# Mamba-2 block with a grouped top-2 mixture of experts: experts and last stage in the same block as the projection, norm rows and eight residual tiles loaded beside the last expert tiles

## Chip, cores, metric

One core of a Trainium2 chip. The metric is the device time of one launch in microseconds; the kernel before was run three times. A profiled execution goes with it.

## What is computed

One decoder layer over 2048 tokens of 1024 features, float32. The part that the change touches is the end of it:

```python
x = layer_norm(ALPHA * x + (1 + g1) * y, ln_g[0], ln_b[0])     # y: the mixer's result times w_out
hm = x * (1 + sc2) + sh2
probs = softmax(hm @ w_router + b_router)                      # 32 experts in 4 groups
# the best group by the sum of its two best; in it the two best experts, gates scaled to sum 1
ye = (silu(hm @ w_gate[e]) * (hm @ w_up[e])) @ w_down[e]       # for both experts of each token
y = gate_a * ye_a + gate_b * ye_b
out = layer_norm(ALPHA * x + (1 + g2) * y, ln_g[1], ln_b[1])
```

Every float32 product is made of three products of rounded parts: a matrix is split into a high part (cast by ScalarE) and a low part (what is left, subtracted by VectorE or GpSimd).

## The kernel before

The program is a row of blocks. In a block each engine (TensorE pe, VectorE dve, ScalarE act, GpSimd pool, and the DMA queue of SyncE, sp) has a list of instructions of its own, with semaphore waits between them written out by hand; at a block's end all engines meet. `stage` (L101) builds a stage and then has GpSimd clear, one by one, every semaphore that the stage took, in a block of its own (`clear_semaphores`, L90). There are three stages.

*Stage 1, `mixer_steps`:* 32 steps of the mixer, then in the same block `out_projection` (L1470). It goes over 16 token tiles of 128. On TensorE a step i does the first half of tile i's product (24 matmuls), the turn of tile i-1 (8 transposes, L1579), the second half, and the router product of tile i-1 (L1591). In the last step the turn comes behind the second half. VectorE's `tile` (L1720 to L1747) scales the product (L1727), adds x (L1731), takes the statistics, and makes the router's input h2 from the normed row (L1745, L1747); GpSimd takes the power for the deviation and makes ALPHA times the normed row (L1554, L1556), which ScalarE stores as the residual tile (L1678, `k.xad`), after which SyncE loads the next tile of x into the same buffer. `choose` is the routing: a chain of some 40 small VectorE instructions with one exponential on ScalarE (`power`), called for tiles 0 to 12 (`choose(0, ...)`) and for 13 to 15. TensorE's `rank` then counts, by products with a triangle and with ones, the place of each token in its expert. The router products of tiles 13 and later write the bank that choose(0) reads, so they wait for it:

```python
if isinstance(j, int) and j >= EARLY:
    pe.wait_ge(p_ready, 1)
```

`p_ready` is counted up by choose's third instruction (L1807).

*Stage 2, `experts`:* VectorE works out the plan from the ranks (L2152, nt_i, and on): which token goes to which place of which tile of 128. TensorE turns it into lists of tokens (L2023). GpSimd gathers the tokens of a tile by indirect DMA (L1945), and for each of 46 tiles TensorE makes gate and up products (L1983), turns the result (L2014) and makes the down product. The weights of an expert come in six pieces of 1 MB (gate 0, 1; up 2, 3; down 4, 5), each with a raw buffer, a high part (L2040, ScalarE) and a low part (L1933; pieces 3 and 5 by GpSimd, the others by VectorE). A piece is loaded again once its low part is made. The results are stored by ScalarE (L2052).

*Stage 3, `output`:* for each of 16 token tiles GpSimd gathers both experts' rows (L2257, two indirect DMAs), SyncE loads the residual tile (L2234), in rings of 8; ScalarE scales and squares, VectorE adds, norms and scales (L2299 to L2332), GpSimd takes the power (rstd, L2267), SyncE stores (L2243). GpSimd issues the 16 gathers of the first 8 tiles ahead of the first power.

Of the kernel before, what the change touches and what calls it, by code (L numbers as in the profile page):

```python
# [47 lines left out]
BY_POOL = (0, 2)  # L48

# [146 lines left out]
def mixer_steps(nc, k, first):  # L196

    with ExitStack() as ctx:
        own = ExitStack()
# [61 lines left out]
        o = projection_buffers(k, ctx, first)  # L261
# [31 lines left out]
        def heads_of(row):  # L293
# [15 lines left out]
                 "t1_done y_done yn_done sq_done xdt_done xend_done xd_done y3 gt ms_done rs_done").split())  # L309
        block = ctx.enter_context(nc.Block())  # L310
# [774 lines left out]
        def _(dve):  # L1085
# [378 lines left out]
        out_projection(nc, k, o, block, first, Tail(  # L1464
            ymm=(ymm, SUBS * STEPS), yn_tr=(yn_tr, 2 * STEPS), y_done=(y_done, 2 * STEPS), gt=(gt, 2 * STEPS),
            yt_out=(yt_out, 2 * STEPS), gm_done=(gm_done, STEPS),
            y_stored=[(y, 32 * STEPS) for y in y_stored]))


def out_projection(nc, k, o, block, first, tail):  # L1470


    sem = k.semaphore
    HALF = YTILES // 2
    w_hi, w_lo, yraw, yhi, ylo, wraw = o.w_hi, o.w_lo, o.yraw, o.yhi, o.ylo, o.wraw
# [8 lines left out]
    row_in, mix = sem("row_in"), sem("mix")  # L1484
    eq = flat[:, 0:NE]
    gs, gh, i1 = (flat[:, (2 * E + n * EGROUPS) * EARLY:(2 * E + (n + 1) * EGROUPS) * EARLY] for n in range(3))
    rb_in, p_ready, exp_done, eq_ready, pos_mm, chain = (sem(n) for n in (
        "rb_in p_ready exp_q eq_ready pos_mm chain_q").split())
    (wr_in, t_done, r_done, bn_done, mv_done, ve_done, rstd_done, nmr_done,
     xn_done, xa_out, ha_done, h2_done, h2_out, tr_done, ht_done, lg_mm, xm_done, xa_done) = (sem(n) for n in (  # L1490
         "wr_in t_done r_done bn_done mv_done ve_done rstd_done nmr_done "
         "xn_done xa_out ha_done h2_done h2_out trh_done ht_done lg_mm xm_done xa_done").split())
    x_in = sem("xo_in")
# [19 lines left out]
    def _(sp):  # L1513
# [30 lines left out]
        loop(sp, step)  # L1544

    @block.gpsimd
    def _(pool):
        def step(i, b):
# [7 lines left out]
            nc.gpsimd.tensor_tensor(r[:], r[:], k.b1[:], ALU.add).then_inc(xa_done, 1)  # L1556

        loop(pool, step)

    @block.tensor  # L1560
    def _(pe):
# [33 lines left out]
        def step(i, b):  # L1595
# [49 lines left out]
    def _(act):  # L1645
# [11 lines left out]
        def step(i, b):  # L1657

            j = i - 1
            if in_loop(j, 0, TT):  # L1660
# [20 lines left out]
            if isinstance(i, int) and i == TT - 2:  # L1681
                power(0, EARLY)
# [7 lines left out]
        act.wait_ge(xa_out, 16 * TT)  # L1690
        act.wait_ge(h2_out, 16 * TT)

    @block.vector
    def _(dve):
# [135 lines left out]

        loop(dve, step, 1)
        choose(1, EARLY, TT - EARLY)
        dve.wait_ge(pos_mm, 2)


def experts(nc, k, first):

    with ExitStack() as ctx:
        sb, ps, sem = k.makers(ctx)
        FQ = FE // P
        GU = 4
        PIECES = GU + 2
        raw = [sb(f"piece_raw{q}", [P, 4, 512]) for q in range(PIECES)]
        hi = [sb(f"piece_hi{q}", [P, 4, 512], F32R) for q in range(PIECES)]
        lo = [sb(f"piece_lo{q}", [P, 4, 512], F32R) for q in range(PIECES)]
        ix = [sb(f"ix{b}", [P, 1], I32) for b in range(2)]
# [118 lines left out]
        def _(pe):  # L1968
# [30 lines left out]
            def step(t, b):  # L1999
# [8 lines left out]
                if in_loop(t, 1):  # L2008
                    down(t - 1)
# [452 lines left out]
```

## Time and profile before

| | us |
|---|---|
| median of 3 runs (lowest, highest) | 2989.3 (2984.44, 2990.38) |
| profiled execution, its own time | 2990.43 |
| its span, first to last instruction | 2988.6 |
| TensorE busy | 2718.9 (91%) |
| VectorE, ScalarE, GpSimd busy | 2218.1, 1315.9, 1489.7 |
| projection, tile 1's products to the last rank | 1542 to 1965 |
| experts, plan to last product | 1975 to 2865 |
| last stage, first gather to last instruction | 2873 to 2983 |

Times in rows are microseconds from the span's start; the duration of a row with a count is that of the group. An "idle before" with a releaser is what the engine waited for. A block's end, a branch and a semaphore clear have no row; they show as a gap on all engines. The semaphores' hardware numbers are given out again in a later stage.

### The profile page before, as it was taken

The page shows a single profiled execution, that of the slowest core. Times are in us where ns is not written, and L with a number is a line of the kernel's source. Part 1 is how long each engine was busy: PE and PEld are TensorE (multiplying, and loading weights), DVE is VectorE, ACT ScalarE, POOL GpSimd, SP SyncE. Part 2 cuts the span into 40 slices and gives each one's busy share as a digit, 9 for nine tenths or more (in the row PEclk, how much of TensorE's full clock was granted, in tenths as well). Part 3 has the DMA queues.
Part 4 walks back from the last instruction along what each step waited for, and adds up shares of the span by engine and source line. Part 5 has one row for each costly group of instructions (what it writes and reads, how often), then busy time and mean ns, then how long its engine had stood idle before and what let it go on. Part 6 is the DMA issues. An engine that isn't in the chain of part 4 may idle for free. (4 is left out here: it accounts for less than half of the span.)

```text
span 2988.6 us, 41030 instructions
## 1 busy us (share of the span) xinstructions
PE 2718.9 (91%) x14603; PEld 2316.1 (77%) x14603; DVE 2218.1 (74%) x2647; ACT 1315.9 (44%) x1655; POOL 1489.7 (50%) x755
## 2 busy tenths in 40 slices
PE   3899999999999999999979999949999999999920
PEld 2688888888889888888868888747888888888820
DVE  7678777777878777887863333458888888888857
ACT  4443333343433333343431111126777777777733
POOL 0133433343343334334432222126899999999963
PEclk9899999999999999999989999959999999999965
DMA  8844544444553544455252322249878869678676
GB/s 271 310 183 145 211 155 171 174 171 161 184 211 137 190 175 165 166 184 197 95 169 106 105 105 105 78 152 373 319 269 293 307 242 341 233 259 288 245 273 247
DMA packets 253185, 610.13 MB, mean 204 GB/s; under 512 B 15968, under 2 KB 98560, under 8 KB 244864
## 3 DMA queue, kind: packets, MB, share of 16 engines
q1 hardware_dynamic: 228208, 525.26, 49.2%
q0 software_dynamic: 11520, 41.95, 3.7%
q10 hardware_dynamic: 13328, 41.21, 3.4%
q8 instruction: 79, 1.29, 0.2%
q14 instruction: 50, 0.41, 0.0%
HBM read 600.75 MB, written 99.89 MB: 234 GB/s over the span
## 5 line engine op out<-in xcount | busy, mean ns | idle before, releaser
L1933 DVE TENSOR_TENSOR piece_lo<-piece_raw,piece_hi 128x2048 fp32r<-128x2048 f32 x187 | 563.3, 3031 | 102.5 <-ACT piece_hi L2040 101.3
L2040 ACT CAST piece_hi<-piece_raw 128x2048 fp32r<-128x2048 f32 x280 | 526.7, 1910 | 217.8 <-issue 77.8
L1933 POOL TENSOR_TENSOR piece_lo<-piece_raw,piece_hi 128x2048 fp32r<-128x2048 f32 x93 | 558.9, 6010 | 34.5 <-ACT piece_hi L2040 32.3
L574 PE MATMUL op<-hm,w_hi 128*128 128x512 f32 x2048 | 533.4, 406 | 45.2 <-DVE hm L1236 45.2
L1110 DVE SCALAR_TENSOR_TENSOR cv<-ub,par,cv 128x512 f32<-128x512 f32 x384 | 381.0, 992 | 157.1 <-ACT cv L833 147.9
L574 PEld LDWEIGHTS op<-hm,w_hi 128*128 128x128 f32 x2048 | 379.8, 190 | 119.5 <-DVE hm L1236 45.2
L524 POOL TENSOR_TENSOR xw<-xw,t 128x512 f32<-128x512 f32 x64 | 98.7, 1543 | 488.6 <-DVE t L1178 488.5
L589 PE MATMUL pz<-wz_hi,hm 128*128 128x256 f32 x2048 | 296.9, 290 | 1.1 <-DVE wz_lo L1088 0.5
L589 PEld LDWEIGHTS pz<-wz_hi,hm 128*128 128x128 f32 x2048 | 266.8, 192 | 7.4 <-DVE wz_lo L1088 3.9
L574 PE MATMUL op<-hm,w_lo 128*128 128x512 f32 x1024 | 254.9, 391 | 0.0
L505 POOL TENSOR_TENSOR xdt<-xw,tab 128x512 f32<-128x512 f32 x64 | 70.4, 1100 | 369.3 <-ACT xw L852 345.1
L574 PEld LDWEIGHTS op<-hm,w_lo 128*128 128x128 f32 x1024 | 192.4, 188 | 42.9
L1983 PE MATMUL gp_e<-piece_lo,xt_hi 128*128 128x512 f32 x368 | 151.7, 412 | 4.1 <-DVE xt_lo L2093 4.1
L1983 PE MATMUL yp<-piece_lo,ht_hi 128*128 128x512 f32 x368 | 150.0, 407 | 6.0 <-DVE ht_lo L2128 6.0
L1945 POOL DMA_INDIRECT xg<-hm,ix x48 | 127.7, 2660 | 39.0 <-POOL ix L1942 39.0
L1983 PE MATMUL gp_e<-piece_hi,xt_hi 128*128 128x512 f32 x368 | 146.8, 399 | 0.0
L1983 PE MATMUL gp_e<-piece_hi,xt_lo 128*128 128x512 f32 x368 | 146.5, 398 | 0.0
L1983 PE MATMUL yp<-piece_hi,ht_lo 128*128 128x512 f32 x368 | 146.1, 397 | 0.0
L1983 PE MATMUL yp<-piece_hi,ht_hi 128*128 128x512 f32 x368 | 145.9, 397 | 0.0
L1983 PE MATMUL up_e<-piece_lo,xt_hi 128*128 128x512 f32 x368 | 145.5, 395 | 0.0
L1983 PE MATMUL up_e<-piece_hi,xt_hi 128*128 128x512 f32 x368 | 145.5, 395 | 0.0
L1550 POOL TENSOR_TENSOR rstd<-ve,negh 128x1 f32<-128x1 f32 x16 | 8.8, 550 | 274.2 <-DVE ve L1740 274.2
(338 smaller groups left out, 5698.2 us busy)
## 6 DMA issues: line engine op xcount, KB each, us to landing
hm<-hm_parts SPq DMA_DIRECT2D x30, 4096.0 KB, 13.9
piece_raw<-in_w_gate SPq DMA_DIRECT2D x94, 1024.0 KB
piece_raw<-in_w_up SPq DMA_DIRECT2D x94, 1024.0 KB
piece_raw<-in_w_down SPq DMA_DIRECT2D x92, 1024.0 KB
decay<-acum_rows SPq DMA_DIRECT2D x32, 1024.0 KB
w_raw<-in_w_in SPq DMA_DIRECT2D x48, 512.0 KB, 7.5
expert_out<-ye ACTq DMA_DIRECT2D x46, 512.0 KB
w_ada_part<-in_w_ada_t SPq DMA_DIRECT2D x32, 512.0 KB, 3.9
```

Of the source, the lines that this page charges most:

```text
L505: nc.gpsimd.tensor_tensor(heads(xdt, h), heads(xw, h), k.tab[:, 0, part].unsqueeze(2).to_broadcast([P, 2 * RH, HD]), ALU.mult).then_inc(xd ...
L524: nc.gpsimd.tensor_tensor(x, x, t1[h][:], ALU.add).then_inc(y3, 1)
L574: mm = nc.tensor.matmul(pj[m % 2][:], wp[m][:, kk, :], hm[b][:, hp, kk, :], start=q == 0, stop=q == 3 * KK - 1)
L589: mm = nc.tensor.matmul(pz[:, (a % 2) * GW:(a % 2 + 1) * GW], hm[b][:, hp, kk, a * P:(a + 1) * P], wp[:, kk, :], start=q == 0, stop=q == 3 ...
L1110: nc.vector.scalar_tensor_tensor(out=cv[m % 2][:], in0=ub[:, m, t:t + SPAN], scalar=par[:, t:t + 1], in1=cv[m % 2][:], op0=ALU.mult, op1=A ...
L1550: nc.gpsimd.tensor_tensor(rstd[:], ve[:], k.negh[:, 0:1], ALU.pow).then_inc(rstd_done, 1)
L1933: v.tensor_tensor(lo[q][:], raw[q][:], hi[q][:].bitcast(F32), ALU.subtract).then_inc(lo_done[q], 1)
L1945: nc.gpsimd.indirect_dma_start(out=xg[b][:], out_offset=None, in_=k.h2d[:], in_offset=bass.IndirectOffsetOnAxis(ap=ix[b][:], axis=0)).then ...
L1983: mm = nc.tensor.matmul(acc[:], l[:, first + kk, :], r[:, kk, :], start=start and kk == 0 and n == 0, stop=stop and kk == 3 and n == 2)
L2040: nc.scalar.copy(hi[q][:], raw[q][:]).then_inc(hi_done[q], 1)
```

## The change

One block holds projection, experts and last stage. Their buffers are placed by hand so that each lies where what was there before is done with, and their semaphores live side by side. The mixer's 93 own semaphores are cleared by GpSimd in tile 1 of the projection, to be given out again to the experts and the last stage; everything is cleared once more at the end of the stage.

- SyncE loads the first tile's six weight pieces once the last product of the projection is done, then the row g2. ScalarE makes their high parts around tile 15 and the routing, VectorE the low parts 0 and 1 ahead of choose(1) and 2 behind it, GpSimd 3 and 5.
- choose(0) moves behind tile 14 on VectorE (from step 14 to step 15), its exponential behind a wait for tile 13's router product on ScalarE.
- The turn of tile 0 on TensorE moves behind the second half of tile 1.
- SyncE loads the last stage's two norm rows and residual tile 0 ahead of the expert loop, tiles 1 to 7 as the last expert tile's low parts free their places. The gathers go once all expert results are stored.

The diff, cut:

```diff
+def output_buffers(k, ctx):
...
+    xa = [sb(f"xa{n}", [P, D]) for n in range(1, OUT_RING)]
...
@@ mixer_steps
+        k.semaphores, kept = own_sems, len(k.used)
...
+        of_mixer = k.used[kept:]
+        k.semaphores = stay
+        out_sems = projection_semaphores(k)
+        own_sems.close()
+        of_experts = ExitStack()
+        x = experts_buffers(k, of_experts)
+        of_experts.close()
+        w = output_buffers(k, ctx)
...
+        experts(nc, k, x, o, w, block, first, out_sems, out)
@@ out_projection, sync
         loop(sp, step)
+        sp.wait_ge(o_mm, 2 * TT)
+        for q in range(x.PIECES):
+            sp.dma_start(x.raw[q][:], first_weights(k, q)).then_inc(x.loaded[q], 16)
+        sp.wait_ge(xm_done, TT)
+        sp.dma_start(x.g2[:], k.adad[3].partition_broadcast(P)).then_inc(x.g2_in, 16)
@@ gpsimd
+            if not in_loop(i, 2) and in_loop(i, 1):
+                for s in of_mixer:
+                    pool.sem_clear(s)
         loop(pool, step)
+        for q in (3, 5):
+            pool.wait_ge(x.hi_done[q], 1)
+            nc.gpsimd.tensor_tensor(x.lo[q][:], x.raw[q][:], x.hi[q][:].bitcast(F32), ALU.subtract
+                                    ).then_inc(x.lo_done[q], 1)
@@ tensor
-            final = isinstance(i, int) and i == TT - 1
-            if before and not final:
+            behind = isinstance(i, int) and i in (1, TT - 1)
+            if before and not behind:
                 turn(i - 1)
             if here:
                 products(b, 1)
-            if final:
+            if behind:
                 turn(i - 1)
@@ scalar
                 act.dma_start(k.h2d[bass.ds(j * P, P), :], h2[:]).then_inc(h2_out, 16)
+                if isinstance(j, int) and j == TT - 1:
+                    first_high(0)
+                    first_high(1)
                 if in_loop(j, 1, TT):
                     act.wait_ge(lg_mm, j)
+                if isinstance(j, int) and j == TT - 2:
+                    power(0, EARLY)
...
                 if isinstance(j, int) and j == TT - 1:
                     power(1, TT - EARLY)
+                    first_high(3)
+                    first_high(2)
...
-            if isinstance(i, int) and i == TT - 2:
-                power(0, EARLY)
+        def first_high(q):
+            act.wait_ge(x.loaded[q], 16)
+            nc.scalar.copy(x.hi[q][:], x.raw[q][:]).then_inc(x.hi_done[q], 1)
...
         loop(act, step, 1)
-        act.wait_ge(xa_out, 16 * TT)
-        act.wait_ge(h2_out, 16 * TT)
+        first_high(5)
+        first_high(4)
@@ vector
             if in_loop(i, 1):
                 tile(i - 1, 1 - b)
+            if isinstance(i, int) and i == TT - 1:
+                choose(0, 0, EARLY)
             if in_loop(i, 1, TT - 1):
                 low(i + 1, 1 - b)
             if not in_loop(i, 1):
                 mix_rows()
-            if isinstance(i, int) and i == TT - 2:
-                choose(0, 0, EARLY)
...
         loop(dve, step, 1)
+        first_low(0)
+        first_low(1)
         choose(1, EARLY, TT - EARLY)
+        first_low(2)
         dve.wait_ge(pos_mm, 2)
@@ experts, sync
+        sp.wait_ge(x_in[0], 16)
+        sp.wait_ge(ids_mm, 1)
+        for row, source in ((w.lng, k.d["ln_g"][1]), (w.lnb, k.d["ln_b"][1])):
+            sp.dma_start(row[:], source.partition_broadcast(P)).then_inc(w.row_in, 16)
+        sp.wait_ge(arrived.xa_out, 16 * TT)
+        sp.dma_start(w.xa[0][:], k.xad[0]).then_inc(w.xa_in[0], 16)
+        last = loop(sp, step)
+        for n in range(1, OUT_RING):
+
+            if n % 2:
+                sp.wait_ge(lo_done[(n - 1) // 2], 2 * last + 3)
+                sp.sem_inc(k.passed, 1)
+            sp.dma_start(w.xa[n][:], k.xad[n]).then_inc(w.xa_in[n], 16)
@@ gpsimd
+        for b in range(2):
+            pool.wait_ge(ye_out[b], 16 * (last + 1))
+            pool.sem_inc(k.passed, 1)
@@ program
-            stage(nc, k, mixer_steps, first)
-            if stop > 2:
-                stage(nc, k, experts, first)
-        if stop > 4:
-            stage(nc, k, output, out)
+            stage(nc, k, mixer_steps, first, out)
```

Where it moves instructions. VectorE behind the low parts of tile 15, before (h and r are the projection's rows, yraw here holds the routing's scores, lgP the router's sums):

```order
L1697 TENSOR_TENSOR ylo1a<-yraw,yhi1a 128x1024 [waits yhi_done]
L1697 TENSOR_TENSOR ylo1b<-yraw,yhi1b 128x1024 [waits yhi_done]
L1805 TENSOR_TENSOR yraw<-lgP,rb 128x416 [waits ylo_done,rb_in,lg_mm]
L1806 TENSOR_REDUCE mx<-yraw 128x13 [waits chain_q]
L1807 TENSOR_TENSOR yraw<-yraw,mx 128x416 [waits chain_q]
L1809 TENSOR_REDUCE sm<-yraw 128x13 [waits exp_q]
```

and in the changed kernel:

```order
L1851 TENSOR_TENSOR h<-op,g 128x512 [waits o_mm]
L1855 SCALAR_TENSOR_TENSOR r<-r,h 128x1024 [waits t_done,xo_in]
L1859 BN_STATS bst<-r 128x6 [waits r_done]
L1859 BN_STATS bst<-r 128x6
L1862 BN_AGGR mv<-bst 128x2 [waits bn_done]
L1864 TENSOR_SCALAR ve<-mv 128x1 [waits mv_done]
L1866 SCALAR_TENSOR_TENSOR nmr<-mv,rstd 128x1 [waits rstd_done]
L1869 TENSOR_TENSOR h<-r,wo_raw 128x1024 [waits xn_done]
L1871 TENSOR_TENSOR h<-h,wo_raw 128x1024 [waits ha_done]
L1929 TENSOR_TENSOR yraw<-lgP,rb 128x416 [waits ylo_done,rb_in,lg_mm]
L1930 TENSOR_REDUCE mx<-yraw 128x13 [waits chain_q]
L1931 TENSOR_TENSOR yraw<-yraw,mx 128x416 [waits chain_q]
```

All ten instructions of tile 14 now stand ahead of the routing, and with them ahead of the third row of it, which counts p_ready.

ScalarE from tile 15's normed row on, before:

```order
L1662 ACTIVATE r<-r,nmr,rstd 128x1024 [waits nmr_done]
L1666 DMA hm<-h 128x1024 [waits h2_out,h2_done]
L1673 COPY h2t<-tp 128x512 [waits trh_done,lg_mm]
L1673 COPY h2t<-tp 128x512 [waits trh_done]
L1687 ACTIVATE yraw<-yraw 128x96 [waits p_ready]
L1678 DMA alpha_x<-r 128x1024 [waits xa_done]
L198 UNCONDITIONAL_BRANCH [waits h2_out,xa_out]
L2034 UNCONDITIONAL_BRANCH [waits barrier_Pool_Activation_PE_DVE_SP_release]
```

and in the changed kernel:

```order
L1777 ACTIVATE r<-r,nmr,rstd 128x1024 [waits nmr_done]
L1781 DMA hm<-h 128x1024 [waits h2_out,h2_done]
L1806 CAST piece_hi<-piece_raw 128x2048 [waits w_loaded0]
L1806 CAST piece_hi<-piece_raw 128x2048 [waits w_loaded1]
L1793 COPY h2t<-tp 128x512 [waits trh_done,lg_mm]
L1793 COPY h2t<-tp 128x512 [waits trh_done]
L1811 ACTIVATE yraw<-yraw 128x96 [waits p_ready]
L1806 CAST piece_hi<-piece_raw 128x2048 [waits w_loaded3]
L1806 CAST piece_hi<-piece_raw 128x2048 [waits w_loaded2]
L1800 DMA alpha_x<-r 128x1024 [waits xa_done]
L1806 CAST piece_hi<-piece_raw 128x2048 [waits w_loaded5]
L1806 CAST piece_hi<-piece_raw 128x2048 [waits w_loaded4]
```

Two casts of weight pieces stand ahead of the copies of the turned tile 15, two between the exponential and the residual store, two behind it.

GpSimd at the end of the program, before (ISA is here a semaphore clear; a name behind "waits" is that of the first semaphore with that number):

```order
L2267 TENSOR_TENSOR rstd<-ve,negh 128x1 [waits stm_done,y_done] x8
L2212 UNCONDITIONAL_BRANCH
L94 UNCONDITIONAL_BRANCH [waits barrier_Pool_Activation_PE_DVE_SP_gather]
L97 ISA x36
L92 UNCONDITIONAL_BRANCH
```

and in the changed kernel:

```order
L2375 TENSOR_TENSOR rstd<-ve,negh 128x1 [waits y_stored0,c_th] x8
L279 UNCONDITIONAL_BRANCH
L95 UNCONDITIONAL_BRANCH [waits barrier_Pool_Activation_PE_DVE_SP_gather]
L98 ISA x221
L93 UNCONDITIONAL_BRANCH
```

The rows of 137 and of 48 clears that stood at the two boundaries are gone; the last one has 221.

## Rows read from the trace of the kernel before

**Rows 1.** Page of the profile, part 1: busy us and share of the span by engine.
```profile
PE 2718.9 (91%) x14603; PEld 2316.1 (77%) x14603; DVE 2218.1 (74%) x2647; ACT 1315.9 (44%) x1655; POOL 1489.7 (50%) x755
```

**Rows 2.** Timeline from 1902 us: start, us, engine, line, operation, count, idle time before.
```profile
1902.72 2.01 PE L1566 MATMUL op<-wo_hi,ylo0b 128*128 128x512 f32 x8
1903.57 0.59 DVE L1805 TENSOR_TENSOR yraw<-lgP,rb 128x416 f32<-128x416 f32 x1
...
1905.56 1.94 PE L1591 MATMUL lgP<-w_router,h2t 128*128 128x32 f32 x16 [0.83 <-DVE yraw L1807]
...
1920.45 1.29 DVE L1727 TENSOR_TENSOR h<-op,g 128x512 f32<-128x512 f32 x2
...
1929.77 1.03 PE L1579 MATMUL tp<-ident,h 128*128 128x128 f32 x8
```

**Rows 3.** Timeline, VectorE in a token tile of the steady state.
```profile
1879.90 0.69 DVE L1727 TENSOR_TENSOR h<-op,g 128x512 f32<-128x512 f32 x1 [0.67 <-PE op L1566]
...
1887.20 1.22 DVE L1747 TENSOR_TENSOR h<-h,wo_raw 128x1024 f32<-128x1024 f32 x1
```

**Rows 4.** Timeline, TensorE after its wait for token tile 0.
```profile
1565.46 1.97 PE L1579 MATMUL tp<-ident,h 128*128 128x128 f32 x8 [11.69 <-DVE h L1747]
...
1567.08 3.76 PE L1566 MATMUL op<-wo_hi,yhi1a 128*128 128x512 f32 x8
```

**Rows 5.** Timeline, from the store of tile 14 to the routing's second half.
```profile
1934.24 0.34 ACTq L1678 DMA_DIRECT2D alpha_x<-r  x1
...
1936.84 0.33 SPq L1529 DMA_DIRECT2D r<-in_x  x1
...
1940.27 1.23 DVE L1731 SCALAR_TENSOR_TENSOR r<-r,h 128x1024 f32<-128x1024 f32 x1 [6.72 <-DMA r<-in_x]
...
1948.05 1.97 PE L1579 MATMUL tp<-ident,h 128*128 128x128 f32 x8 [2.68 <-DVE h L1747]
1949.26 0.59 ACT L1673 COPY h2t<-tp 128x512 f32<-128x512 f32 x1 [3.78 <-PE tp L1579]
...
1954.35 0.26 DVE L1805 TENSOR_TENSOR yraw<-lgP,rb 128x96 f32<-128x96 f32 x1 [6.36 <-PE lgP L1591]
...
1963.57 0.16 DVE L1829 TENSOR_TENSOR gate_b<-gate_b,sm 128x3 f32<-128x3 f32 x1
```

**Rows 6.** Page, part 5: weight casts of ScalarE, busy and mean ns.
```profile
L2040 ACT CAST piece_hi<-piece_raw 128x2048 fp32r<-128x2048 f32 x280 | 526.7, 1910 | 217.8 <-issue 77.8
```

**Rows 7.** Line L1933 (ns min/median/max), then timeline rows of VectorE beside GpSimd.
```profile
L1933 DVE TENSOR_TENSOR piece_lo<-piece_raw,piece_hi x187: 2274/2293/6660, 1992.2 to 2851.9; 128x2048 fp32r<-128x2048 f32 x187
L1933 POOL TENSOR_TENSOR piece_lo<-piece_raw,piece_hi x93: 4517/5817/6662, 2003.5 to 2854.0; 128x2048 fp32r<-128x2048 f32 x93
...
1417.05 0.89 DVE L1100 COPY ub<-ub 128x3 f32<-128x3 f32 x1
...
2065.56 4.04 DVE L1933 TENSOR_TENSOR piece_lo<-piece_raw,piece_hi 128x2048 fp32r<-128x2048 f32 x1 [0.20 <-ACT piece_hi L2040]
```

**Rows 8.** Timeline, last row of the projection's block and first of the experts'.
```profile
1964.03 1.04 PE L1637 MATMUL op<-yraw,ones 128*128 128x32 f32 x4
...
1975.05 0.19 DVE L2152 TENSOR_SCALAR nt_i<-op 128x32 int32<-128x32 f32 x1 [11.32 <-PEq L92]
```

**Rows 9.** Timeline, TensorE in the first expert tile.
```profile
2024.98 0.83 PE L2014 MATMUL hp_e<-ident,h_e 128*128 128x128 f32 x4 [2.89 <-DVE h_e L2118]
```

**Rows 10.** Last stage: timeline; busy by engine, clock, DMA, GB/s; waits (us, times, longest).
```profile
2866.11 0.34 ACTq L2052 DMA_DIRECT2D expert_out<-ye  x1
...
2873.09 0.96 POOL L2257 DMA_INDIRECT ya<-expert_out,slot_a  x1 [12.58 <-PEq L2212]
...
2894.10 0.60 POOL L2267 TENSOR_TENSOR rstd<-ve,negh 128x1 f32<-128x1 f32 x1
...
2894.00:2945.00 51.00, 0.00 (x0) 0.00 (x0) 42.27 (x57) 18.12 (x25) 29.42 (x26) 0.50 1.03 415
...
DVE o L2326 <- DMA out<-o: 5.7, 7, 1.3
```

More of the change, by code:

```diff
@@ L48 @@
 BY_POOL = (0, 2)
+OUT_RING = 8
 def in_loop(i, low=0, high=1 << 30):
@@ L198, in mixer_steps, with first_weights @@
+def first_weights(k, q):
+    if q < 4:
+        return k.d["w_gate" if q < 2 else "w_up"][0].rearrange("(kk p) f -> p kk f", p=P)[:, (q % 2) * 4:(q % 2) * 4 + 4, :]
+    return k.d["w_down"][0].rearrange("(kk p) f -> p kk f", p=P)[:, :, (q - 4) * 512:(q - 3) * 512]
+def mixer_steps(nc, k, first, out):
     with ExitStack() as ctx:
-        own = ExitStack()
+        own, later, own_sems = ExitStack(), ExitStack(), ExitStack()
+        stay = k.semaphores
         sb, ps, sem = k.makers(own)
@@ L1462, in _ @@
             low_y(1, 1)
-        out_projection(nc, k, o, block, first, Tail(
+        out_projection(nc, k, o, x, out_sems, of_mixer, block, first, Tail(
             ymm=(ymm, SUBS * STEPS), yn_tr=(yn_tr, 2 * STEPS), y_done=(y_done, 2 * STEPS), gt=(gt, 2 * STEPS),
@@ new lines, in experts, with loop, _, load @@
+def experts(nc, k, x, o, w, block, first, arrived, out):
+    FQ, GU, PIECES = x.FQ, x.GU, x.PIECES
+    raw, hi, lo, ix, xg, ye, g2 = x.raw, x.hi, x.lo, x.ix, x.xg, x.ye, x.g2
+    xt_hi, xt_lo, ht_hi, ht_lo, th, a, h = x.xt_hi, x.xt_lo, x.ht_hi, x.ht_lo, x.th, x.a, x.h
+    E = EXPERTS
+    nt_i, lp_i, nt, end, base, cmp = x.nt_i, x.lp_i, x.nt, x.end, x.base, x.cmp
+    slf, pf, tf, sl_i, p_i, t_i, tok1, before, te = x.slf, x.pf, x.tf, x.sl_i, x.p_i, x.t_i, x.tok1, x.before, x.te
+    cand, pm, marks = th[:], a[:], x.marks
+    lanes = [[t[:].rearrange("p (t q) -> p t q", q=P) for t in pair] for pair in (xg, ye)]
+    xp = first
+    position, total = first
+    gp, up, hp, yp = x.gp, x.up, x.hp, x.yp
+    loaded, hi_done, lo_done, used = x.loaded, x.hi_done, x.lo_done, x.used
+    sem = k.semaphore
+    ids_ready, ids_mm, lanes_done, marks_done, te_done, te_mm, table_ready, chain = (sem(n) for n in (
+        "ids_ready ids_mm lanes_done marks_done te_done te_mm table_ready chain_d").split())
+    x_in = [sem(f"xg_in{b}") for b in range(2)]
+    ye_out = [sem(f"ye_out{b}") for b in range(2)]
+    (ix_ready, x_tr, xt_hi_done, xt_lo_done, th_done, a_done, h_done, h_tr, ht_hi_done, ht_lo_done, ye_done) = (
+        sem(n) for n in ("ix_ready x_tr xt_hi_done xt_lo_done the_done a_done h_done h_tr ht_hi_done ht_lo_done "
+                         "ye_done").split())
+    def loop(eng, step):
+        eng.wait_ge(table_ready, 1)
+        last = eng.value_load(k.last_pair[0:1, 0:1], min_val=TT - 1, max_val=MAXT // 2 - 1)
+        step(0, 0)
+        step(1, 1)
+        with eng.Fori(1, last + 1) as q:
+            step(2 * q, 0)
+            step(2 * q + 1, 1)
+        return last
+    @block.sync
+    def _(sp):
+        def load(t, pieces):
+            if in_loop(t, 1):
+                e = sp.value_load(k.tile_expert[0:1, bass.ds(t, 1)], min_val=0, max_val=EXPERTS - 1)
+                fresh = sp.value_load(k.fresh[0:1, bass.ds(t, 1)], min_val=0, max_val=1)
+            else:
+                e = 0
+            for q in pieces:
+                if q < GU:
+                    w = k.d["w_gate" if q < 2 else "w_up"][bass.ds(e, 1)]
+                    w = w.rearrange("e (kk p) f -> p (e kk) f", p=P)[:, (q % 2) * 4:(q % 2) * 4 + 4, :]
+                else:
+                    w = k.d["w_down"][bass.ds(e, 1)]
+                    w = w.rearrange("e (kk p) f -> p (e kk) f", p=P)[:, :, (q - GU) * 512:(q - GU + 1) * 512]
```

881 lines of the change are left out of this document (434 added, 447 removed).

## Prediction

> **What bounds the kernel now.** I read the page first, then the timeline around the two places where the program goes from one block to the next, then the waits and the busy time by stage of the last stage. TensorE is busy 91% of the span [rows 1], in the mixer, the projection and the expert tiles, and nothing of that arithmetic changes. What changes lies in three stretches where TensorE is not the bound: the last two token tiles of the projection with the routing (1903 to 1975 us), the start of the experts (1975 to 2028), and the last stage (2866 to the end). I take them in turn, against the profiled execution: span 2988.6, its own time 2990.43, which is 1.1 above the median of the runs, 2989.3.
>
> **How the routing runs before.** The first half of the routing (choose(0), 13 tiles) stands on VectorE ahead of tile 14. It begins at 1903.57; TensorE's router product for tile 13 (L1591) waits for its third instruction and starts at 1905.56, having lost 0.8 us [rows 2]. VectorE reaches tile 14 only at 1920.45, but TensorE runs through the products of tile 15 meanwhile and turns tile 14 at 1929.77 [rows 2]. So the 17 us of routing lie beside 24 us of TensorE work.
>
> **The change, part by part.**
>
> *1. choose(0) behind tile 14.* TensorE's wait on p_ready ahead of the router product of tile 13 is still there, and p_ready now comes from an instruction that stands behind all of tile 14 on VectorE. Products of tile 14 end at 1904.73 [rows 2]. A tile in the steady state takes VectorE from its second L1727 to the end of L1747: 1879.90 to 1888.42, 8.5 us [rows 3]; so tile 14 is done at 1904.8 + 8.5 = 1913.3. From the first routing instruction to TensorE's start were 2.0 us [rows 2]. Some 1 us comes on top, since GpSimd multiplies and adds tile 14's row just then (part 3). TensorE starts at 1916.2 instead of 1905.56: +10.7. Queued behind that wait are tile 15's two halves of products, the turn of tile 14, its router product, the ranks of 13 tiles, the turn of tile 15. After the wait TensorE is slow: after 11.69 us of idle time eight transposes took 1.97 us, against 1.03, and eight products 3.76, against 2.01 [rows 2, 4]; nearly twice as long, as at the lower level of 1.2 GHz; it cost about 2.7 us there. Turn of tile 14: 1929.77 + 13.4 = 1943.2.
>
> From there two paths lead to the turn of tile 15. The ranks ended 15.6 us after the turn of tile 14 began (1929.77 to 1948.05 - 2.68 = 1945.37, since TensorE had idled 2.68 us ahead of the turn of tile 15): 1958.8. The other: ScalarE's two copies and its store of tile 14 come behind that turn, then the load of x for tile 15 waits for the store. Before, from the store at 1934.24 to VectorE's L1731 were 6.0 us, and from there to the turn of tile 15 7.8 [rows 5]; now the store goes at 1943.2 + 1.8 = 1945.0, L1731 at 1951.0, the turn at 1958.8. Both give 1958.8 against 1948.05: **+10.8**. [rows 2, 5]
>
> *2. Two weight casts between on ScalarE.* first_high(0) and (1) stand behind the store of tile 15's h2 and ahead of the two copies that the last router product needs. The first copy came 1.2 us after the turn began [rows 5]; now it comes after an issue (0.3) and two casts of 1.91 [rows 6], 4.1 us: **+2.8**. The weights (loaded behind the last product, and behind x of tile 15) should be there, so no more. choose(1) starts at 1954.35 + 13.6 = 1968.0.
>
> *3. First low parts.* VectorE's first two (2.29 each, the median in rows 7) fit into its wait for the router product: nothing. GpSimd's two become ready at about 1971 and 1975.2, one on top of choose(1) (1968.0, and 9.4 us long, rows 5). In the trace VectorE and GpSimd do not share here: a VectorE low part that met one of GpSimd's took 4.04 us instead of 2.29, and a copy of 3 columns beside a GpSimd instruction 0.89 us [rows 7], where 32 columns take 0.19 with GpSimd at rest [rows 8]. The Trainium skill ("SBUF — State Buffer", Who interferes with whom) has it that a VectorE instruction with two SBUF inputs and a GpSimd one that reads SBUF lock each other out for a whole instruction, and that a reduce never does; by this rule too the links with two inputs wait, and the trace agrees for the low parts. choose(1) is a chain of some 40 links, most with two inputs. I charge it GpSimd's two instructions nearly whole, 4.5 us each (the shortest, rows 7): +8.7; bounds 0 and 9.0. Then first_low(2) stands between it and the first link of the plan: **+2.3**. The plan (nt_i) starts at 1968.0 + 9.4 + 8.7 + 2.3 = 1988.4. Before, it started at 1975.05 [rows 8]. So although the first boundary is gone, the plan is late by **+13.3** (bounds: no lock-out, full speed after the wait and 1 us less wait, +1; all of it and 3 us of load contention, +16). The chain from nt_i to the first expert product is the same instructions; the low parts taken out of it lay beside TensorE's marks products.
>
> *4. First expert tile.* TensorE lost 2.89 us ahead of L2014 [rows 9], since VectorE's low parts waited for the up pieces, whose load waited for the last low part. All four pieces are now asked for at once, but behind two rows and a residual tile. **-2.5**; bounds -3.5 and +2.
>
> *5. Second boundary and last stage.* The last expert store is issued at 2866.11, the first gather at 2873.09 [rows 10]. A store's landing takes about 2.6 us (the store at 1934.24 had released the next load by 1936.84), so the gather can go at 2868.9: -4.2. The first rstd does not wait for data but for the 16 gathers ahead of it on GpSimd (2873.09 to 2894.10, rows 10), so loading the residuals early brings no more than 1 us here. After it 51 us go at 415 GB/s with the DMA engines full [rows 10], and VectorE waited 5.7 us for out stores [rows 10]. With 5.2 MB fewer (8 tiles and 2 rows of 0.52 MB) queued ahead, nearly all of this wait goes: -5.8. Sum **-11**; bounds -7 and -13.
>
> *6. Semaphores.* GpSimd clears 137 of them at the first boundary and 48 at the second, 36 at the end; now 93 in tile 1 of the projection, where GpSimd idles 15 us, and 221 at the end. The clears are not dropped but moved there, 185 of them. Last TensorE row to first VectorE row: 1965.07 to 1975.05, 10.0 us with 137 clears; store landed to gather, 2868.7 to 2873.09, 4.4 us with 48 [rows 8, 10]. The difference, 5.6 us over 89, is 0.063 each; all of 10.0 over 137 is 0.073. I take 0.067: **+12.3**, nothing beside it; bounds 11.7 and 13.4. The Trainium skill ("Runtime: NRT & Kernel Launch", The ~15µs preamble/postamble breakdown) gives about 1.5 us for 51 resets on an engine. By that price, an estimate of 0.03 each, the sum would be 7 us less; the boundary rows speak for mine.
>
> *7. Turn of tile 0 behind the second half.* TensorE's 11.69 us of waiting [rows 4] goes, but the low parts of tile 2 hang on the loads, and TensorE waits for them instead, some 10 us, and is slow after that: 0, bounds -1 and +1.
>
> Sum: +13.3 - 2.5 - 11 + 12.3 = **+12.1 us**, 0.4%: 3002.5 for such an execution, 3001 beside the median.
>
> **Rivals.**
> *A, the lock-out doesn't reach the small links.* For it: they are 0.2 us long, the rows show mostly long ones. Then part 3 is 8.7 less: +3.4, 2993.
> *B, the clears at the end are cheap or lie beside something,* the boundaries having been dear for their restarts. Against it: two boundaries with 137 and 48 clears differ by 5.6 us. Between nothing and the page's price: -0.2 to +5, 2989 to 2994.
> *C, the other side: the reordering pays.* Place: the p_ready wait at L1591. If TensorE is not held there long (VectorE reaches its third routing instruction early), tile 14 runs 15 us sooner and tile 15's x loads sooner, and the first boundary's 10 us are gained whole, with nothing lost to the casts: 12.3 - 2.5 - 11 - 10 = -11, 2978. It decides for faster once the plan starts before about 1970, that is if all of parts 1 to 3 cost under 5 us. Against it: the order of waits leaves no way round tile 14.
> *D, the boundary is not crossed any sooner than the data allow,* so that the last stage gains only its 4 us: +19, 3008.
>
> **Chances.** Forecast 0.58, A 0.13, B 0.13, C 0.10, D 0.06. Predicted 3001. The forecast's own range is 2994 to 3008; with A and most of B the range is 2987 to 3009. A measurement of this kernel can tell about 0.2%, 6 us, from no change: slower by more 0.68 (the forecast's cases, D, a little of B), within it 0.21 (A and B), faster 0.11.
>
> **What would show it.** TensorE idle some 10 us ahead of the router product of tile 13, the turn of tile 15 near 1959, choose(1) stretched where GpSimd's low parts run, nt_i near 1988; the gathers 2.8 us after the last expert store; a last stage at 5.5 us per tile from its first rstd on; and some 18 us, most of them clears, between VectorE's last instruction and the end of the span. I am wrong if the plan starts before 1980, or if that last stretch is under 10 us.

## Result: 0.8% slower, and the profile after

The changed kernel takes 3011.18 us (median of 4 runs, 3009.38 to 3012.38) beside 2986.95 us of the kernel before (4 runs, 2984.44 to 2990.38): ratio 1.0081, 95% interval 1.0066 to 1.0096. A second comparison, with other runs of both, gave 1.0068 (1.0054 to 1.0081). The forecast was slower by 12.1 us; it is 20.5 us between the two profiled executions (spans 2988.6 and 3009.1), and 24.2 us between the medians, since the profiled execution of the kernel before stands 3.5 us above its median of 4; in the second comparison the medians, 3010.89 and 2991.69, are 19.2 us apart. The time lies above the range of 2987 to 3009.

The page's first part of the changed kernel stands against [rows 1]: no engine has more instructions there, and VectorE's 5.4 us more are instructions that took longer, so the 20 us are waits, stretched instructions and clears.

```profile
span 3009.1 us, 41086 instructions
...
PE 2719.6 (90%) x14603; PEld 2317.6 (77%) x14603; DVE 2223.5 (74%) x2647; ACT 1314.7 (44%) x1655; POOL 1491.6 (50%) x755
```

Lines have new numbers: L1706 is the router product (L1591 before), L1694 the turn (L1579), L1929 to L1953 the routing, L2272 the plan's first instruction, L1672 GpSimd's first low parts, L2434 and L2440 the last stage's L2326 and L2332. The timeline, TensorE alone, from the turn of tile 13 to the last router product, answers to [rows 2, 5]:

```profile
1893.09 1.03 PE L1694 MATMUL tp<-ident,h 128*128 128x128 f32 x8
...
1916.57 1.67 PE L1706 MATMUL lgP<-w_router,h2t 128*128 128x32 f32 x7 [11.34 <-DVE yraw L1931]
...
1943.88 1.03 PE L1694 MATMUL tp<-ident,h 128*128 128x128 f32 x8
...
1959.21 1.09 PE L1694 MATMUL tp<-ident,h 128*128 128x128 f32 x8 [1.47 <-DVE h L1871]
1964.29 3.62 PE L1706 MATMUL lgP<-w_router,h2t 128*128 128x32 f32 x16 [3.99 <-ACT h2t L1793]
```

TensorE idles 11.34 us ahead of the router product of tile 13, and both turns come where the prediction had them (1943.2 and 1958.8). The 3.99 us in the last row were 0.68 before; the two weight casts add 3.3.

The routing's second half, VectorE and then GpSimd:

```profile
1970.92 0.26 DVE L1912 TENSOR_REDUCE yraw<-cand 128x12 f32<-128x96 f32 x1
1971.22 4.41 DVE L1913 TENSOR_SCALAR yraw<-yraw 128x12 f32<-128x12 f32 x1
1975.66 4.51 DVE L1914 TENSOR_TENSOR oh<-tidx,yraw 128x96 f32<-128x96 f32 x1
```

```profile
1971.09 8.97 POOL L1672 TENSOR_TENSOR piece_lo<-piece_raw,piece_hi 128x2048 fp32r<-128x2048 f32 x2 [7.28 <-ACT piece_hi L1806]
```

Two links of 0.17 and 0.26 us take 4.41 and 4.51, one beside each of GpSimd's two low parts.

The start of the experts, SyncE's queue, and TensorE at the end of the first tile [rows 9]:

```profile
2017.99 0.34 SPq L2034 DMA_DIRECT2D lng<-in_ln_g  x1
2018.38 0.43 SPq L2034 DMA_DIRECT2D lnb<-in_ln_b  x1
2018.86 0.68 SPq L2036 DMA_DIRECT2D xa<-alpha_x  x1
2021.82 1.12 SPq L2022 DMA_DIRECT2D piece_raw<-in_w_gate  x2
2023.37 4.51 SPq L2022 DMA_DIRECT2D piece_raw<-in_w_up  x2
```

```profile
2041.55 1.11 PE L2134 MATMUL hp_e<-ident,h_e 128*128 128x128 f32 x4 [5.91 <-DVE h_e L2238]
```

The wait that was to go has doubled, from 2.89 to 5.91 us. TensorE has a second wait, ahead of the second tile's first product, before and in the changed kernel:

```profile
2028.54 0.79 PE L1983 MATMUL gp_e<-piece_lo,xt_hi 128*128 128x512 f32 x1 [2.73 <-DVE xt_lo L2093]
```

```profile
2043.02 0.80 PE L2103 MATMUL gp_e<-piece_lo,xt_hi 128*128 128x512 f32 x1 [0.36 <-DVE xt_lo L2213]
```

The two together were 5.62 us and are 6.27.

The second boundary and the last stage, from the last expert store on; the 51 us behind the first rstd by engine, with clock, DMA share and GB/s; the wait for out stores; VectorE's last instruction [rows 10]:

```profile
2880.05 0.34 ACTq L2172 DMA_DIRECT2D expert_out<-ye  x1
2883.45 0.96 POOL L2365 DMA_INDIRECT ya<-expert_out,slot_a  x1 [8.80 <-DMA expert_out<-ye]
...
2903.40 0.59 POOL L2375 TENSOR_TENSOR rstd<-ve,negh 128x1 f32<-128x1 f32 x1
...
2903.40:2954.40 51.00, 0.00 (x0) 0.00 (x0) 44.35 (x59) 18.24 (x24) 32.39 (x25) 0.50 0.99 369
...
DVE o L2434 <- DMA out<-o: 3.0, 4, 0.9
...
2987.62 1.28 DVE L2440 SCALAR_TENSOR_TENSOR o<-o,rstd,lnb 128x1024 f32<-128x1024 f32 x1 [0.73 <-POOL rstd L2375]
```

The gather comes 3.4 us after the store's issue (7.0 before), the DMA engines move 369 GB/s instead of 415, VectorE still waits 3.0 us for out stores (5.7 before), and its last instruction ends at 2988.90, 20.2 us ahead of the span's end (6.0 before).

### The profile page after: what moved, and what is told of

Same layout as the page of the kernel before. It is cut to its first block, busy times and chain, and to the rows that moved or that the text cites. A ratio compares the mean times of both kernels' runs of the same rounds, so it can differ in the third digit from the quotient of the medians.

```text
span 3009.1 us, 41086 instructions
## 1 busy us (share of the span) xinstructions
PE 2719.6 (90%) x14603; PEld 2317.6 (77%) x14603; DVE 2223.5 (74%) x2647; ACT 1314.7 (44%) x1655; POOL 1491.6 (50%) x755
## 4 chain that ended last, share of the span: by engine, by line
PE 76%; DVE 9%; issue 5%; DMA 3%; POOL 3%; ACT 2%; SPq 1%; ACTq 0%; POOLq 0%; DVEq 0%
PE op L666 18%; PE op L1681 11%; PE pz L681 10%; PE gp_e L2103 9%; PE yp L2103 8%; PE up_e L2103 8%; DVE cv L1202 3%; PE yi L725 3%; PE yx L728 2%; PE op L2095 1%; PE sbp L733 1%; PE tx L744 1%; PE lgP L1706 1%; DVE decay L1239 1%; PE tx L698 1%
## 5 line engine op out<-in xcount | busy, mean ns | idle before, releaser
L2051 DVE TENSOR_TENSOR piece_lo<-piece_raw,piece_hi 128x2048 fp32r<-128x2048 f32 x184 | 550.4, 3009 | 113.9 <-ACT piece_hi L2160 113.8
L2160 ACT CAST piece_hi<-piece_raw 128x2048 fp32r<-128x2048 f32 x274 | 514.9, 1909 | 190.6 <-issue 79.1
L2051 POOL TENSOR_TENSOR piece_lo<-piece_raw,piece_hi 128x2048 fp32r<-128x2048 f32 x91 | 552.4, 6072 | 40.5 <-ACT piece_hi L2160 39.1
L2103 PE MATMUL up_e<-piece_hi,xt_lo 128*128 128x512 f32 x368 | 145.7, 396 | 0.0
```

Of the source, the lines that this page charges most:

```text
L2051: v.tensor_tensor(lo[q][:], raw[q][:], hi[q][:].bitcast(F32), ALU.subtract).then_inc(lo_done[q], 1)
L2103: mm = nc.tensor.matmul(acc[:], l[:, first + kk, :], r[:, kk, :], start=start and kk == 0 and n == 0, stop=stop and kk == 3 and n == 2)
L2160: nc.scalar.copy(hi[q][:], raw[q][:]).then_inc(hi_done[q], 1)
```

## The stretches of all kernels

The mixer's part of the program, up to the turn of tile 13, took between 1886.6 and 1894.3 us in the fourteen traces of this case, with the same instructions in it but for the 93 clears and the place of one turn in the changed family. A difference of two spans can be off by that. So the traces are compared by the stretches behind that turn; these are their lengths, from the timelines, in us. The columns: to the routing's second half; to the plan's first instruction; to the first expert product; to the first product of the second expert tile; to the end of the last product; to the first gather; to the first rstd; to the end of VectorE's last instruction; to the span's end.

| kernel | routing 2 | plan | product | tile 2 | last product | gather | rstd | VectorE | end |
|---|---|---|---|---|---|---|---|---|---|
| before | 61.8 | 20.7 | 33.1 | 20.4 | 836.7 | 7.9 | 21.0 | 88.5 | 6.0 |
| changed | 75.0 | 20.1 | 33.2 | 21.6 | 836.1 | 4.3 | 20.0 | 85.5 | 20.2 |
| changed, again | 74.6 | 20.1 | 33.2 | 22.2 | 835.7 | 4.3 | 20.1 | 86.6 | 20.2 |
| e1 routing back | 64.5 | 20.1 | 33.3 | 22.3 | 835.7 | 4.3 | 20.2 | 85.6 | 20.2 |
| e2 low parts late | 74.7 | 11.0 | 33.2 | 22.0 | 837.7 | 4.3 | 20.3 | 85.6 | 20.2 |
| e3 weights first | 74.6 | 20.1 | 33.2 | 18.3 | 836.1 | 4.3 | 20.3 | 85.8 | 20.3 |
| e4 clears once | 74.5 | 20.1 | 33.3 | 22.6 | 837.7 | 4.3 | 20.4 | 86.2 | 14.2 |
| e5 before, routing late | 71.0 | 20.7 | 33.1 | 20.5 | 836.2 | 7.9 | 20.8 | 88.5 | 6.0 |
| e6 before, clears added | 61.9 | 20.7 | 33.1 | 20.6 | 837.7 | 7.9 | 21.2 | 88.4 | 18.1 |
| e7 three output tiles | 74.5 | 20.1 | 33.0 | 21.2 | 836.5 | 4.3 | 20.3 | 82.0 | 20.3 |
| e8 casts behind | 71.5 | 20.2 | 33.6 | 22.5 | 837.7 | 4.3 | 20.2 | 84.8 | 20.2 |
| e10 before, clears shared | 61.8 | 14.5 | 33.1 | 20.4 | 838.4 | 5.9 | 20.9 | 88.1 | 4.5 |
| e11 half the residuals | 74.5 | 20.1 | 33.1 | 22.4 | 835.7 | 4.3 | 20.2 | 85.5 | 20.2 |
| e9 best | 61.9 | 11.0 | 33.2 | 17.8 | 834.5 | 4.3 | 20.5 | 82.0 | 8.5 |

Where nothing was done to them, the columns up to the first product and those of the gather, the rstd and the end repeat to 0.6 us within the changed family and within that of before. The second tile (21.2 to 22.6), the expert loop (834.5 to 838.4) and the last stage (84.8 to 86.6) spread more.

## The experiments

### The routing's first half back (e1), and moved alone (e5)

```diff
-            if isinstance(i, int) and i == TT - 1:
-                choose(0, 0, EARLY)
             if in_loop(i, 1, TT - 1):
                 low(i + 1, 1 - b)
             if not in_loop(i, 1):
                 mix_rows()
+            if isinstance(i, int) and i == TT - 2:
+                choose(0, 0, EARLY)
```

with power(0, EARLY) on ScalarE moved likewise. e5 is the reverse edit in the kernel before.

> The change with its first part undone: the first half of the routing and its exponential stand again where they stood before, ahead of tile 14; all else as changed. Theory (the moved routing holds TensorE at the router product of tile 13): that product starts near 1905.6 instead of 1916.6, the turn of tile 15 comes near 1948 instead of 1959.2, and the whole run is 10.8 us shorter than the changed kernel, 3000.4. Rival (something else holds tile 15, such as the weight loads now in this stretch): under 3 us shorter.

> The kernel before with one thing changed: the first half of the routing and its exponential stand behind tile 14, as in the change; blocks, loads and semaphores as before. Theory (the move costs by itself what it costs in the change): TensorE idles some 11 us ahead of the router product of tile 13 and the run is 10.8 us longer than before. Rival (the move pays or is free by itself, and only the merged block makes it dear): within 3 us of before.

Measured: e1 2999.27 us, ratio to before 1.0033 (1.0021 to 1.0045), against 1.0081 and 1.0068 of the changed kernel; e5 2999.36, ratio 1.0028 (1.0017 to 1.0039), 7.7 us above the median of before, 2991.69. TensorE's rows ahead of the router product of tile 13, e1's and then e5's:

```profile
1907.38 1.94 PE L1706 MATMUL lgP<-w_router,h2t 128*128 128x32 f32 x16 [0.94 <-DVE yraw L1931]
```

```profile
1914.42 1.88 PE L1591 MATMUL lgP<-w_router,h2t 128*128 128x32 f32 x8 [11.34 <-DVE yraw L1807]
```

The same wait of 11.34 us stands in e5, without any merged block: the move costs this by itself. In e1 the routing's second half is 10.1 to 10.5 us sooner. In e5 it is 9.2 us later than before: the turn of tile 15 is 11.7 us later, and 2.4 come back, since TensorE does not idle ahead of that turn and does the last router product in 1.97 us.

### Low parts out of the routing (e2), casts behind it (e8)

e2 takes out GpSimd's loop over pieces 3 and 5 and VectorE's first_low(2), and puts them into the experts' part:

```diff
+        pool.wait_ge(te_done, 1)
+        first_low(3)
...
         fetch(0, 0)
         fetch(1, 1)
+        first_low(5)
...
+        dve.wait_ge(hi_done[2], 1)
+        v.tensor_tensor(lo[2][:], raw[2][:], hi[2][:].bitcast(F32), ALU.subtract).then_inc(lo_done[2], 1)
         dve.wait_ge(ids_mm, 1)
```

e8 moves first_high(0) and first_high(1) behind power(1, ...), and VectorE's low parts 0 and 1 to the same place ahead of the ids_mm wait.

> The change with GpSimd's two low parts and VectorE's third one taken out of the routing: GpSimd does one while TensorE sums the marks and one behind the first gathers, VectorE does its third while it waits for the token ids. Theory (the two engines shut each other out, and the third low part stands in the way): the second half of the routing takes 9.4 us instead of 18, the plan starts 11 us sooner (8.7 and 2.3) and the run is 11 us shorter, 3000. Rival A (no lock-out; those links are slow for another reason): only the 2.3 us of the third low part. Rival B (the low parts, now late, hold the first expert tile): the plan is early but the first product is not, under 5 us.

> The change with ScalarE's first two weight casts behind the last copies and the exponential instead of ahead of them, and VectorE's first two low parts in its wait for the token ids; GpSimd's low parts stay where they are. Theory (the casts hold the copies): from the turn of tile 15 to the second half of the routing 6.3 us instead of 8.9, the plan 2.5 us sooner. Rival (GpSimd's low parts come later too, and meet longer instructions, the plan's, instead of the routing's small ones): the plan gains more, as the lock-out leaves the routing, and loses it again behind nt_i; the run within 3 us of the changed kernel.

Measured: e2 3002.93 us, ratio 1.0045 (1.0031 to 1.0059). The second half of the routing takes 9.4 us, and the plan comes 9.1 us sooner, not 11:

```profile
1974.49 0.16 DVE L1949 TENSOR_TENSOR gate_b<-gate_b,sm 128x3 f32<-128x3 f32 x1
1976.31 0.19 DVE L2274 TENSOR_SCALAR nt_i<-op 128x32 int32<-128x32 f32 x1 [1.65 <-PE op L1748]
```

The plan now waits 1.65 us for TensorE's last ranks. In the changed kernel the third low part lay beside that wait, so of its 2.3 us only some 0.6 were on the path. The lock-out has only moved to where it costs nothing, the wait for the token ids (VectorE, then GpSimd, in the timeline of e2):

```profile
1993.26 4.53 POOL L2070 TENSOR_TENSOR piece_lo<-piece_raw,piece_hi 128x2048 fp32r<-128x2048 f32 x1 [32.24 <-DVE te L2313]
1993.27 0.14 DVE L2315 TENSOR_SCALAR last_pair<-lp_i 1x1 int32<-1x1 int32 x1
1993.44 6.49 DVE L2317 TENSOR_TENSOR piece_lo<-piece_raw,piece_hi 128x2048 fp32r<-128x2048 f32 x1
```

e8: 3007.13 us, ratio 1.0053 (1.0038 to 1.0069). The routing's second half begins 3.1 to 3.5 us sooner. GpSimd's low parts come sooner too (the first at 1968.69), and hit two other links:

```profile
1968.72 4.52 DVE L1912 TENSOR_SCALAR sm<-sm 128x3 f32<-128x3 f32 x1
1973.27 4.42 DVE L1913 TENSOR_TENSOR yraw<-tidx,sm 128x12 f32<-128x12 f32 x1
```

So in these two traces the charge of two low parts does not depend on which links they meet. The theory held, and the rival did not: the plan's column stays at 20.2. Of the 3 us 2.1 are left at the second tile's first product and only 0.4 behind the last product, since the expert loop was 1.6 us longer than in the changed kernel's first trace, which is within its spread.

### Weights of tile 1 first (e3)

The three loads into lng, lnb and xa[0], with their waits, stand behind `last = loop(sp, step)` instead of ahead of it.

> The change with the two norm rows and the first residual tile loaded behind the expert loop's weights instead of ahead of them. Theory (1.5 MB and three issues ahead of the weights of tile 1 cost what the earlier low parts had won): the weights are asked for 1.5 us sooner and arrive some 3 us sooner behind the first gather, TensorE's wait ahead of the transposes of h falls from 5.9 to 2 us or less, and the run is 3.8 us shorter, 3007.4. Rival (that wait is set by something else, such as the low parts of VectorE in a row): 1.5 us or less. The last stage should not change by more than 1 us.

Measured: 3004.29 us, ratio 1.0047 (1.0033 to 1.0061). SyncE's queue, and TensorE at the end of the first tile:

```profile
2017.90 1.08 SPq L2022 DMA_DIRECT2D piece_raw<-in_w_gate  x2
2019.12 1.59 SPq L2022 DMA_DIRECT2D piece_raw<-in_w_up  x2
```

```profile
2035.88 0.65 PE L2134 MATMUL hp_e<-ident,h_e 128*128 128x128 f32 x4 [2.58 <-DVE h_e L2238]
```

The wait is 2.58 instead of 5.91 us, and the second tile starts 3.3 to 3.9 us sooner than in the changed kernel; the last stage is unchanged. Behind the first gather the gate pieces are asked for after 6.8 us, as before, instead of 8.4, and the first cast starts 6.2 us after that, where it waits for TensorE, instead of 9.4, where it waited for the load. So the three loads, 1.5 MB, cost this much by their issue and by their bytes. The two waits of TensorE are 2.58 and 0.84 us here, 3.42 together, and the second tile starts 2.0 us sooner than before: without the three loads part 4 of the prediction would have come out near its -2.5. The median fell by more, 6.9 us; the stretches do not show the rest, and e11, all of whose stretches are those of the changed kernel, has a median 3.7 us lower too.

### Clears: once (e4), added to the kernel before (e6), shared (e10)

e4 leaves the 93 semaphores of the mixer out of the list at the end. e6 adds 185 clears behind the 36 of the kernel before. e10 shares the lists of the kernel before over four engines:

```diff
-            for s in k.used:
-                pool.sem_clear(s)
+            for s in k.used[0::4]:
+                pool.sem_clear(s)
...
+        @block.vector
+        def _(dve):
+            for s in k.used[1::4]:
+                dve.sem_clear(s)
```

and likewise for ScalarE and SyncE.

> The change with 128 semaphores cleared at the end instead of 221: the 93 that are cleared in the projection are not cleared again. Theory (0.077 us for each on GpSimd, from 14.2 us over 185): 7.2 us shorter, 3004, and 13.0 instead of 20.2 us between VectorE's last instruction and the end. By the price of the Trainium skill (Runtime: NRT & Kernel Launch, The ~15us preamble/postamble breakdown), an estimate of 0.03 each, it would be 2.8 us. Rival (the long end is another cost of the one large block): no change.

> The kernel before with 185 more semaphore clears on GpSimd behind the last 36, so that 221 stand at the end as in the changed kernel; nothing else. Theory (a clear has a price of its own, 0.064 to 0.077 us): 12 to 14 us longer than before, 18 to 20 us between VectorE's last instruction and the end. By the price of the Trainium skill (Runtime: NRT & Kernel Launch, The ~15us preamble/postamble breakdown), an estimate of 0.03 each, 5.5 us longer. Rival (clears are near free, and the merged block's end is long for another reason): under 2 us.

> The kernel before with its three lists of clears (137, 48 and 36) shared out over GpSimd, VectorE, ScalarE and SyncE; nothing else. It tells what of the best version's gain needs the merged block. Theory (0.066 us for each clear, three quarters of them taken off GpSimd): 6.7 us at the first boundary, 2.4 at the second, 1.8 at the end, 11 us in all, 2980. Rival (the other engines clear more slowly, or a boundary is made of other waits): under 5 us.

Measured: e4 3004.16 us, ratio 1.0051 (1.0037 to 1.0064); e6 3005.17, ratio 1.0050 (1.0037 to 1.0064); e10 2979.27, ratio 0.9965 (0.9952 to 0.9979). VectorE's last instruction in e4 (span 3002.2) and in e6 (span 2998.8):

```profile
2986.69 1.28 DVE L2442 SCALAR_TENSOR_TENSOR o<-o,rstd,lnb 128x1024 f32<-128x1024 f32 x1 [0.73 <-POOL rstd L2377]
```

```profile
2979.38 1.28 DVE L2334 SCALAR_TENSOR_TENSOR o<-o,rstd,lnb 128x1024 f32<-128x1024 f32 x1 [0.73 <-POOL rstd L2269]
```

The last column falls by 5.97 us for 93 clears and rises by 12.16 for 185: 0.064 and 0.066 us each, on GpSimd. The Trainium skill's 1.5 us for an engine's 51 resets behind a kernel (Runtime: NRT & Kernel Launch, The ~15µs preamble/postamble breakdown), an estimate of 0.03 each, is under half of what these traces show. e10 gains 6.2, 2.0 and 1.5 us at the two boundaries and the end, and its median is 10.5 us lower: at 0.064 us each the 137 clears are 8.8 of the first boundary's 10.0 us and the 48 are 3.1 of the second's 4.4, so most of what a boundary costs here is one engine's clears, not the restart.

### The last stage: three output tiles (e7), half the residuals (e11)

e7 gives the last stage a third tile o, with a third store semaphore, so that a tile is written again only three tiles later. e11 leaves out `load(i + R)`, the residual loads of tiles 8 to 15.

> The change with three output tiles instead of two in the last stage; nothing else. Theory (with 5.2 MB fewer queued, VectorE still waits 3.0 us for stores that are under way, every second tile; half a tile more of slack takes that away): from the first rstd to VectorE's last instruction 82 to 83 us instead of 85.5, the run 3 us shorter. Rival (the gathers and residual loads are then late instead): no change.

> The change without the residual loads of tiles 8 to 15 in the last stage (4.2 MB left out; those tiles add the residual of the tile eight places ahead). Theory (VectorE's remaining wait for out stores is the load of the DMA engines): the 3.0 us go, as with three output tiles. Rival (it is the length of one store, whatever else is queued): they stay.

Measured: e7 3007.64 us, ratio 1.0060 (1.0045 to 1.0075); e11 3007.5, ratio 1.0059 (1.0043 to 1.0074). In e7 no wait for an out store is left, and the stretch from rstd to VectorE's end is 82.0 us. In e11 the waits of the last stage still hold this row:

```profile
DVE o L2434 <- DMA out<-o: 3.2, 3, 1.4
```

With 4.2 MB fewer under way the wait stays, with one more tile it goes. So the residual loads of tiles 8 to 15 are not its cause. The load of the DMA engines as such is not excluded: in the changed kernel the first eight out stores land 5.5 to 6.3 us after their issue (median 6.0), in e11 4.9 to 6.8 (6.1), and in both the later ones, with the gathers done, take 2.6 (median of the last eight). The waits all lie ahead of 2953 and of 2944, while gathers are still under way; the DMA engines are 83% busy in e11's 51 us behind the first rstd, at 285 GB/s. A store in that traffic is too long for two output tiles, and a store by itself is not. No run takes the gathers out, so that they are what stretches it is not shown.

### The changed kernel again (e0), and the costs taken out (e9)

> The changed kernel once more, beside the others on one chip: 3011 us, and the same stretches as in its first profile to within 0.5 us each, except where the DMA queues decide (the first expert tiles, the last stage).

> The merged block with its costs taken out: the routing's first half back where it was; the casts of the first weights behind the exponential, VectorE's low parts in its wait for the token ids, GpSimd's behind the first gathers; norm rows and residual tiles behind the expert loop's weights; the 93 semaphores not cleared twice and the other 128 shared out over GpSimd, VectorE, ScalarE and SyncE; three output tiles instead of two in the last stage. Theory, from the terms measured so far: 10.5 for the routing, 9.4 to 11 for the low parts, 2.8 for the casts, 3.5 for the weights, 6 for the 93 clears, some 6 for the sharing, 1 to 2 for the third tile: 39 to 41 us under the changed kernel, 2970 to 2972, and faster than the kernel before by 0.5%. Rival (the terms hide each other, the wait for the ranks or the data take their place): above 2980.

Measured: e0 3010.89 us, ratio 1.0068 (1.0054 to 1.0081). e9 puts together the edits of e1, e3, e4 and e7 and the later casts of e8, puts GpSimd's low parts behind the first gathers and VectorE's three into its wait for the ids, and shares the last 128 clears over four engines: **2967.24 us, ratio 0.9923 (0.9909 to 0.9936), 24.5 us faster than the kernel before** and 43.7 faster than the changed one in the same comparison. The stretches add up to 41 to 43 us: 12.7 to 13.1 from the routing and the casts, 9.1 from the low parts, 3.8 to 4.4 from the weights, 3.5 to 4.6 from the third tile, 11.7 at the end. Of the 24.5 us 10.5 can be had without merging anything (e10, in another comparison); what a third output tile brings in the kernel before was not run.

## Why the prediction was right and wrong

The direction was right, and so were the mechanisms of parts 1 to 3 and of the clears. Three terms of the sum were mis-sized, all to the same side: part 4, which came out with the other sign, the last stage from the first rstd on, and the end. Together they are 8.5 us; between forecast and measurement lie 8.4. In the two profiled executions, term by term (0.5 of the first row stand ahead of the turn of tile 13, in the mixer's spread; the stretch from the plan to the first product adds 0.1):

| part | predicted | measured | shown by |
|---|---|---|---|
| 1 to 3: plan late | +13.3 | +13.1 | e1, e5, e2, e8 |
| 4: first expert tile | -2.5 | +1.3 | e3 |
| expert loop | 0 | -0.5 | not told from its spread |
| 5: gather after last product | -4.2 | -3.6 | |
| 5: first rstd after gather | -1 | -1.1 | |
| 5: last stage from rstd | -5.8 | -3.0 | e7, e11 |
| 6: end | +12.3 | +14.2 | e4, e6 |
| sum | +12.1 | +20.5 | |

- **Parts 1 to 3** came to within 0.7 us at each step: TensorE at 1916.57 (1916.2 predicted), the two turns, the second half at 1968.08 (1968.0), the plan at 1988.18 (1988.4). Rival A is excluded by e2 and e8. The two links that were hit lost 8.5 us; one of them has a single input, where the prediction had reckoned with links of two. The 1.8 us from the turn of tile 14 to the store stand in no row (there it was 4.5, since GpSimd had made the row only then); they were 1.1. One piece of the working was wrong without showing: the third low part was charged 2.3 us and cost 0.6, since the ranks would have held the plan anyway (e2); the casts were charged 2.8 and cost a little more (e8: 3.1 to 3.5).
- **Part 4 is the step that failed most**, by 3.8 us. "All four pieces are now asked for at once, but behind two rows and a residual tile: -2.5" took the gain of the early low parts and only named the 1.5 MB ahead. The gate pieces were asked for 1.5 us later after the first gather than before, and their first cast waited until 2031.17, 9.4 us after the issue. e3 takes the three loads away and gets 3.3 to 3.9 us. It also reckoned with one of TensorE's two waits at this place: of 5.62 us together it took 2.89. The upper bound of +2 held the value; choosing near the lower end was the mistake.
- **Part 5**: "with 5.2 MB fewer queued ahead, nearly all of this wait goes". Of 5.7 us 3.0 stayed (and -5.8 was already more than the wait). The step that failed is that the residual loads and rows were nearly the whole cause: e11 takes 4.2 MB more away, and the wait is 3.2 us. With two output tiles a store of some 6 us still holds VectorE; e7's third tile takes the whole wait, and its 82.0 us are 6.5 under the 88.5 of before. What makes a store that long while gathers run stays open.
- **Part 6**: the price per clear, 0.067, was right (0.064 and 0.066). Some 2 us more stand at the end of the merged kernel and belong to no clear: e4 with 128 clears has 14.2 us, and 92 clears more than the 6.0 us of before make 12.0; e6 with 221 clears in the kernel before has 18.1, the changed kernel with as many 20.2. No run tells what they are; this stays open. Rival B is excluded by e6.
- **Part 7** (the turn of tile 0) cost nothing that can be seen: 1892.6 and 1893.1 us up to the turn of tile 13, within the mixer's own spread.
- **Rival C** is excluded. VectorE did reach tile 14 16.5 us sooner (1903.93 instead of 1920.45), but TensorE was held to 1916.57, turned the tile at 1943.88, 14 us later than before, and the plan started at 1988.18. Rival D said the last stage would gain only 4 us; it gained 7.7. D's total, +19, lies nearest the 20.5, but by luck: its extra 7 us stand in the last stage, the measured ones in three places.
- **The range** was built from the terms' bounds and not from the spread of the executions. The mixer alone spreads over 7.7 us, and the profiled execution of before stood 3.5 us above the median that the result is compared with.

## What to carry to other kernels

An early load is free only if nothing on the path is queued behind it: put what is needed 800 us later behind what is needed now, even if it is three small loads. Merging two blocks saves the restart, but what a boundary costs may be one engine's clearing of semaphores; that can be shared over the engines without merging anything (10.5 us here, e10), and semaphores cleared on the way need no second clear. Work moved into a pause of one engine must be held against the other engine that shares its path: a pause on GpSimd is no free place while VectorE runs a chain of small links.

## What the runs showed of the hardware

A link's size does not shield it from GpSimd: VectorE instructions of 3 and 12 columns, 0.17 us long alone, took 4.52 us (e8) and 4.41 us (the changed kernel) beside a GpSimd low part of 4.5 us, nearly its whole length. The Trainium skill (SBUF — State Buffer, Who interferes with whom) says that tensor_scalar can take the shared pair in some modes and that whoever issues second is blocked for the whole instruction; the trace agrees for these two, which are both tensor_scalar. One semaphore clear on GpSimd costs 0.065 us (e4, e6), and four engines clear at the same time (e10: 6.2 us less at the boundary with 137). A store of 0.5 MB lands 2.6 us after its issue when little else is under way and some 6.0 us after it beside gathers and loads (changed kernel, medians of the last and the first eight out stores).
